# Decoder trunk of two layers: the last expert block chosen by 0/1 products while earlier rows are gathered, and conditioning ahead of the low weight parts at the start

## The chip, the cores and the metric

The kernel runs on one core of a Trainium2 chip. The metric is the device time of one execution in microseconds (us), as the median of several runs. A core has a matrix engine (TensorE, "PE" in the profile, its weight loads "PEld"), three engines for elementwise work (VectorE "DVE", ScalarE "ACT", GpSimd "POOL"), a queue engine (SyncE, "SP") and 16 DMA engines between device memory and the on-chip memory. Every engine runs its own list of instructions in order; they meet only through semaphores.

## The reference

Only what matters here is kept: two layers; each layer conditions its input with a row worked out from `c`, mixes tokens, and then passes them through a feed-forward part, which in the second layer is the mixture of experts.

```python
D_MODEL = 1024; SEQ = 512; DEPTH = 2; N_EXPERTS = 8; TOP_K = 2; D_FF_EXPERT = 1024

def modulate(x, g, shift, scale):
    return rmsnorm(x, g) * (1.0 + scale[:, None, :]) + shift[:, None, :]

def moe_ffn(h, router_w, router_b, w_gate, w_up, w_down):
    t = h.reshape(B * S, D)
    logits = (t @ router_w).astype(jnp.float32) + router_b.astype(jnp.float32)
    top_v, top_i = lax.top_k(logits, TOP_K)
    top_p = jax.nn.softmax(top_v, axis=-1)
    combine = jnp.sum(jax.nn.one_hot(top_i, N_EXPERTS) * top_p[..., None], axis=1)
    for e in range(N_EXPERTS):
        out = out + combine[:, e:e + 1] * swiglu(t, w_gate[e], w_up[e], w_down[e])

def reference(x, c, positions, ada_w, ada_b, ...):
    c_act = jax.nn.silu(c)
    for l in range(DEPTH):
        mod = jnp.einsum('bd,kde->kbe', c_act, ada_w[l]) + ada_b[l][:, None, :]
        ...
        h = modulate(x, norm_mix_g[l], sh1, sc1)
        x = x + gt1 * token_mixer(h, ...)
        h = modulate(x, norm_ffn_g[l], sh2, sc2)
        x = x + gt2 * (swiglu(h, ...) if l % 2 == 0 else moe_ffn(h, ...))
    return rmsnorm(x, final_norm_g)
```

## The kernel before

**Precision.** A float32 product is made of three products of a cheaper type: each operand is split into a high part (a rounded copy, by ScalarE) and a low part (operand minus high part, by VectorE), and TensorE adds high x high, high x low and low x high. The weights are split as they arrive, so each weight tile passes DMA, ScalarE, VectorE and TensorE.

**The opening.** SyncE loads `x`, constants and eight 1 MB groups of `ada` (the conditioning weights), then the first two tiles of `w_in` into `raw`. TensorE multiplies the groups with `cact` as they land (`condition_rows`, line 617, `condition_sum`, line 625); after the eighth, VectorE adds the bias (`modulation`, into `mod` and `sclg`). ScalarE then writes the high part `hhi` of the conditioned `h` and VectorE the low part `hlo`, chunk by chunk (eight chunks of 128 features). VectorE's order is: the low parts of weight tiles 0 and 1 (`split`, line 1755), `modulation`, then eight times {the whole value by line 1850, minus `hhi` by line 1745}. TensorE's `first_pair` (lines 668 to 670) waits for both low weight parts and then follows `h_ready` chunk by chunk, for tiles 0 and 1 together. GpSimd works out rotary angles at the same time (lines 552 to 565).

**The experts.** Each token goes to 2 of 8 experts. VectorE works out for each of the 512 x 2 choices a row number (`slots`) in a buffer `xs` of 15 blocks of 128 rows (NB = 15). GpSimd scatters the token rows there by eight indirect DMAs (line 572), waits for all of them (`xs_done`) and loads block 1 into `xg` (line 575); block 0 is built on the chip by products with 0/1 columns (`first_slots`, line 1183). For each block, TensorE turns `xg` (eight transposes, `slots_in`, line 1210, in the middle of the block before it, at tile t = 20), and works through 24 half-megabyte weight tiles, two at a time (12 pairs): 8 pairs of gate and up products, 4 pairs of down products, 12 products of 128x512 to a pair (lines 1248 to 1250). ScalarE copies the high parts three pairs ahead (`high`, line 1358), but not before TensorE is done with the pair three earlier (`hi_pair` has three places); VectorE follows with the low parts (`low`, into `wlm`). Between them VectorE does `times`, `hidden`, `tokens` and `results`. `results` multiplies the block's output by the gate row `grow` and writes it to `yb`; SyncE stores `yb` to rows of `ys` in device memory (line 502) between the weight loads at t = 20 of the next block, and after the last load for the last block. SyncE's weight loads wait until VectorE is done with the tile twelve earlier.

**The end.** After the last block GpSimd waits for the last store and gathers 2 rows for each token from `ys` by eight indirect DMAs (line 582, into `rawm`, token chunks c = 0 to 3, two each). For each chunk ScalarE multiplies the first row by its share (`weighted`, line 1691), VectorE adds the second times its share (line 1748) and the residual (line 1745, turned into token order by `residual_in_tokens`), ScalarE takes the root (`root`, lines 1697 and 1698), VectorE normalizes (`normed`, lines 2311 and 1748), TensorE turns it back (`out_turned`, line 1257), ScalarE copies it out (`turned_back`, line 1704) and SyncE stores it (line 526).

## Time and profile before

| | us |
|---|---|
| median of 3 runs | 1572.52 |
| lowest and highest of them | 1568.59, 1574.78 |
| the profiled execution's own time | 1571.0 |
| its span, first to last instruction | 1568.9 |

| engine | busy us | share of the span |
|---|---|---|
| PE | 1510.3 | 96% |
| PEld | 1203.1 | 77% |
| DVE | 1161.9 | 74% |
| ACT | 787.1 | 50% |
| POOL | 64.1 | 4% |

The page cuts the span in 40 slices; PE has 5 tenths in the first, 3 in the last and 9 nearly everywhere between. The experts' stage is the stretch from about 1014 us to 1532 us, and what follows it runs to the end at 1568.9. How to read a row of a timeline: start in us, duration in us, engine, line, operation, output<-inputs, shape, how many (merged), and in brackets how long the engine had been idle before it and what ended that.

### The profile page before, as it was taken

The page shows a single profiled execution, that of the slowest core. Times are in us where ns is not written, and L with a number is a line of the kernel's source. Part 1 is how long each engine was busy: PE and PEld are TensorE (multiplying, and loading weights), DVE is VectorE, ACT ScalarE, POOL GpSimd, SP SyncE. Part 2 cuts the span into 40 slices and gives each one's busy share as a digit, 9 for nine tenths or more (in the row PEclk, how much of TensorE's full clock was granted, in tenths as well). Part 3 has the DMA queues.
Part 4 walks back from the last instruction along what each step waited for, and adds up shares of the span by engine and source line. Part 5 has one row for each costly group of instructions (what it writes and reads, how often), then busy time and mean ns, then how long its engine had stood idle before and what let it go on. Part 6 is the DMA issues. An engine that isn't in the chain of part 4 may idle for free.

```text
span 1568.9 us, 22626 instructions
## 1 busy us (share of the span) xinstructions
PE 1510.3 (96%) x9030; PEld 1203.1 (77%) x9030; DVE 1161.9 (74%) x1425; ACT 787.1 (50%) x927; POOL 64.1 (4%) x50
## 2 busy tenths in 40 slices
PE   5999999999999999999999999899999999999993
PEld 3667877778888888886688778688888888888883
DVE  4879866676666665446578765689999999999984
ACT  3534246242222222224542364677777777777774
POOL 8200000000000000000000000200000000000001
PEclk9999999999999999999999999999999999999996
DMA  9453211446555554531211005399999999999975
GB/s 356 138 209 108 82 41 60 155 148 199 187 183 183 185 189 150 183 109 54 68 50 50 26 28 187 112 415 410 396 399 397 400 389 395 393 392 403 397 273 174
DMA packets 94599, 340.33 MB, mean 217 GB/s; under 512 B 10016, under 2 KB 14240, under 8 KB 91808
## 3 DMA queue, kind: packets, MB, share of 16 engines
q1 hardware_dynamic: 92048, 329.99, 57.2%
q0 software_dynamic: 2448, 8.91, 1.5%
q8 instruction: 71, 1.16, 0.3%
q14 instruction: 32, 0.26, 0.0%
HBM read 316.85 MB, written 22.02 MB: 216 GB/s over the span
## 4 chain that ended last, share of the span: by engine, by line
PE 88%; DVE 4%; DMA 4%; issue 1%; ACT 1%; POOL 1%; SPq 0%; POOLq 0%; DVEq 0%; ACTq 0%
PE ps L654 34%; PE ps L1250 10%; PE ps L1248 10%; PE ps L1249 10%; PE ps L964 2%; DMA scr<-in_ada 2%; PE ps L992 1%; DVE scr L1748 1%; PE ps L818 1%; PE ps L810 1%; PE ps L976 1%; DMA xs<-sq,slots 1%; PE ps L606 1%; PE ps L1076 1%; PE ps L1077 1%
## 5 line engine op out<-in xcount | busy, mean ns | idle before, releaser
L1745 DVE TENSOR_TENSOR wlm<-rawm,hlo 128x2048 fp32r<-128x2048 f32 x120 | 274.6, 2289 | 16.8 <-ACT hlo L1358 15.6
L1289 ACT ACTIVATE whi<-raw 128x1024 fp32r<-128x1024 f32 (+1 forms) x112 | 123.6, 1103 | 305.0 <-PE ps L654 260.3
L1358 ACT ACTIVATE hlo<-rawm 128x2048 fp32r<-128x2048 f32 x120 | 230.2, 1919 | 72.2 <-PE ps L1250 72.2
L654 PE MATMUL ps<-hhi,whi 128*128 128x512 f32 x624 | 252.2, 404 | 1.3 <-DVE wlo L1755 1.3
L1755 DVE TENSOR_TENSOR wlo<-raw,whi 128x1024 fp32r<-128x1024 f32 (+1 forms) x112 | 144.1, 1287 | 143.2 <-ACT whi L1289 141.0
L654 PE MATMUL ps<-hlo,whi 128*128 128x512 f32 x624 | 243.6, 390 | 0.0
L654 PE MATMUL ps<-hhi,wlo 128*128 128x512 f32 x624 | 243.6, 390 | 0.0
L1249 PE MATMUL ps<-wlm,xgh 128*128 128x512 f32 x480 | 186.8, 389 | 0.0
L1745 DVE TENSOR_TENSOR wlm<-rawm,whm 128x2048 fp32r<-128x2048 f32 x60 | 137.4, 2291 | 25.7 <-ACT whm L1358 25.7
L654 PEld LDWEIGHTS ps<-hhi,whi 128*128 128x128 f32 x624 | 117.3, 188 | 38.1 <-issue 12.6
L1248 PE MATMUL ps<-hlo,xgh 128*128 128x512 f32 x360 | 141.6, 393 | 1.5 <-ACT xgh L1667 1.5
L1250 PE MATMUL ps<-hlo,xgl 128*128 128x512 f32 x360 | 140.3, 390 | 0.0
L654 PEld LDWEIGHTS ps<-hhi,wlo 128*128 128x128 f32 x624 | 117.3, 188 | 25.7
L654 PEld LDWEIGHTS ps<-hlo,whi 128*128 128x128 f32 x624 | 117.5, 188 | 23.4 <-issue 1.0
L1358 ACT ACTIVATE whm<-rawm 128x2048 fp32r<-128x2048 f32 x60 | 115.0, 1916 | 17.1 <-PE ps L1250 17.1
L1249 PEld LDWEIGHTS ps<-wlm,xgh 128*128 128x128 f32 x480 | 90.2, 188 | 18.3
L1748 DVE SCALAR_TENSOR_TENSOR adas<-adah,cact,adas 128x256 f32<-128x256 f32 x196 | 94.9, 484 | 6.6
L1249 PE MATMUL ps<-wlm,hih 128*128 128x512 f32 x240 | 93.5, 390 | 0.0
L1748 DVE SCALAR_TENSOR_TENSOR scr<-scr,par 128x511 f32<-128x511 f32 (+26 forms) x120 | 82.8, 732 | 1.5
L1248 PEld LDWEIGHTS ps<-hlo,xgh 128*128 128x128 f32 x360 | 67.6, 188 | 15.2 <-ACT xgh L1667 1.6
L1250 PEld LDWEIGHTS ps<-hlo,xgl 128*128 128x128 f32 x360 | 67.6, 188 | 14.3
L654 PE MATMUL ps<-ghi,whi 128*128 128x512 f32 x176 | 69.3, 394 | 0.0
(327 smaller groups left out, 2534.5 us busy)
## 6 DMA issues: line engine op xcount, KB each, us to landing
rawm<-in_wm SPq DMA_DIRECT2D x360, 512.0 KB, 8.0
raw<-in_w SPq DMA_DIRECT2D x96, 512.0 KB, 3.6
adah<-in_ada SPq DMA_DIRECT2D x56, 512.0 KB, 4.4
scr<-in_ada SPq DMA_DIRECT2D x20, 1024.0 KB, 6.0
raw<-in_w SPq DMA_DIRECT2D x16, 704.0 KB, 4.2
xs<-scr SPq DMA_DIRECT2D x15, 512.0 KB, 5.7
ys<-yb SPq DMA_DIRECT2D x15, 512.0 KB, 8.9
xg<-xs SPq DMA_DIRECT2D x13, 512.0 KB, 7.5
```

Of the source, the lines that this page charges most:

```text
L606: ins = pe.matmul(ps[:, 7, 2 * g + m:2 * g + m + 1], ada_sum_in(g)[:, m * P:m * P + P], C("ones")[:, 0:1], start=True, stop=True)
L654: ins = pe.matmul(ps[:, b, :], a, r[:, k0 + k, :], start=(start and first and k == ks[0] and n == 0), stop=(stop and last and k == ks[-1] ...
L810: ins = pe.matmul(ps[cr, 2 + u // 8, u % 8 * 64:u % 8 * 64 + 64], cmp(MT)[cr, u, :], cmp(TC)[cr, u, :], start=True, stop=True)
L964: ins = pe.matmul(ps[:, b, c * 256 + lo:c * 256 + 256], QT[2 * b + c][r, n * P:(n + 1) * P], KT[r, (n - 1) * P + lo:(n + 1) * P], start=Tr ...
L1248: pe.matmul(ps[:, bank, :], ah[:, k, :], w_hi, start=(k == 0), stop=False)
L1249: pe.matmul(ps[:, bank, :], ah[:, k, :], w_lo, start=False, stop=False)
L1250: ins = pe.matmul(ps[:, bank, :], al[:, k, :], w_hi, start=False, stop=(k == DC - 1))
L1289: act.activation(whi[:, slot, 0:width], raw[:, slot, 0:width], ACT.Copy).then_inc(sem("hi_ready"), 1)
L1358: act.activation(hi_pair(q), raw_pair(q), ACT.Copy).then_inc(sem("him_ready"), 1)
L1745: return dve.tensor_tensor(out, a, b, op)
L1748: return dve.scalar_tensor_tensor(out=out, in0=a, scalar=s, in1=b, op0=op0, op1=op1)
L1755: dve.tensor_tensor(wlo[:, slot, 0:width], raw[:, slot, 0:width], whi[:, slot, 0:width].bitcast(F32), ALU.subtract).then_inc(sem("lo_ready ...
```

## The change

There are two parts. In the opening, VectorE does `modulation` first and takes the low part of weight tile 0 behind the first chunk of `hlo` and that of tile 1 behind the second; `first_pair` waits for high and low weight parts where it first uses each. At the end:

- The routing shares are put into slot order, so that `results` can multiply by them: after the eight scatters, GpSimd scatters 8 x 128 single values into `share` (device memory), loads block 1 as before, waits for the shares and loads them as `pslot` (128x16). TensorE's `slots_in(1)` waits for both loads (`xg_first` at 32).
- The last block's rows of `ys` are zeroed at the start of the kernel and never stored. The block before it is stored at t = 13 of the last block instead of t = 20.
- GpSimd gathers as soon as 14 blocks are stored, straight into `htok`, the second row of each token by a DMA that adds.
- The last block's rows are picked on the chip: VectorE makes 0/1 columns (`first_choice`, `second_choice`), TensorE turns them at t = 20, and `rows(c)` adds for each chunk the products `picked` x `yb` and the residual's transposes in the same bank. `combine` is then one addition.

```diff
@@ the sync engine, opening
+                    if t == 0:
+                        sp.dma_start(share.rearrange("(p n) o -> p (n o)", p=P), ZERO[:, 0:16])\
+                            .then_inc(sem("xs_cleared"), 16)
+                        sp.dma_start(ys[(NB - 1) * P:NB * P, :], ZERO).then_inc(sem("xs_cleared"), 16)
@@ the sync engine, expert blocks
-                    if b and t == 20:
+                    if b and t == (20 if b < NB - 1 else 13):
                         store_slots(b - 1)
...
-            store_slots(NB - 1)
@@ gpsimd, after the eight scatters
+            pool.wait_ge(sem("p_ready"), 1)
+            for c in range(4):
+                for k in range(2):
+                    pool.indirect_dma_start(share[:], bass.IndirectOffsetOnAxis(ap=sidx[:, k, c:c + 1], axis=0),
+                                            rt[:, 64 + 4 * k + c:65 + 4 * k + c], None).then_inc(sem("share_out"), 16)
             pool.wait_ge(sem("xs_done"), 8 * 16)
             pool.dma_start(xg[:, 1, :], xs[P:2 * P, :]).then_inc(sem("xg_first"), 16)
-            low_done(pool, NB * NT - 1)
+            pool.wait_ge(sem("share_out"), 8 * 16)
+            pool.dma_start(pslot[:], share.rearrange("(s b) o -> s (b o)", s=P)).then_inc(sem("xg_first"), 16)
             for parity in range(2):
-                pool.wait_ge(sem(f"y_out{parity}"), 16 * ((NB + 1 - parity) // 2))
-            for c in range(4):
-                for k in range(2):
-                    pool.indirect_dma_start(yg[:, c, k, :], None, ys[:],
...
+                pool.wait_ge(sem(f"y_out{parity}"), 16 * ((NB - parity) // 2))
+            for pair in range(2):
+                for k, c in [(k, 2 * pair + q) for k in range(2) for q in range(2)]:
+                    if k:
+                        pool.wait_ge(sem(f"yg_in{c}"), 16)
+                    pool.indirect_dma_start(htok[:, c, :], None, ys[:],
+                                            bass.IndirectOffsetOnAxis(ap=slots[:, k, c:c + 1], axis=0),
+                                            compute_op=ALU.add if k else ALU.bypass).then_inc(sem(f"yg_in{c}"), 16)
@@ tensor, first_pair
-                pe.wait_ge(sem("lo_ready"), g + 2)
...
+                    if k == 0:
+                        pe.wait_ge(sem("hi_ready"), g + j + 1)
                     pe.matmul(ps[:, j, :], w_hi, hhi[:, k, :], start=(k == 0), stop=False)
                     pe.matmul(ps[:, j, :], w_hi, hlo[:, k, :], start=False, stop=False)
+                    if k == 0:
+                        pe.wait_ge(sem("lo_ready"), g + j + 1)
@@ tensor, experts
-                            pe.wait_ge(sem("xg_first"), 16)
+                            pe.wait_ge(sem("xg_first"), 32)
...
                                 if b + 1 < NB:
                                     slots_in(b + 1)
+                                else:
+                                    feature_row(PR("fg", 0, DC), 0)
+                                    slots_turned()
@@ tensor, the end (residual_in_tokens goes)
+                    def rows(c):
+                        for half in range(2):
+                            if c == 0:
+                                pe.wait_ge(sem("y_ready"), NB + half)
+                            pe.matmul(ps[:, 2 * c + half, :], picked[:, c * P:(c + 1) * P],
+                                      yb[:, 0, half * S:(half + 1) * S], start=True, stop=False)
+                            for k in range(4 * half, 4 * half + 4):
+                                ins = pe.matmul(ps[:, 2 * c + half, (k % 4) * P:(k % 4) * P + P],
+                                                x[:, k, c * P:(c + 1) * P], C("ident"), start=False, stop=(k % 4 == 3))
+                        ins.then_inc(sem("htok_done"), 1)
@@ scalar, the end: weighted(c) goes, and turned_rows of the four residual chunks
+                    act.activation(picked, ps[:, 4, :], ACT.Copy).then_inc(sem("htok_ready"), 1)
@@ vector, opening
-            for g in range(2):
-                split(g)
             dve.wait_ge(sem("ada_used"), G_IN)
             modulation(0, 2 * G_IN, 0, 1)
...
+            shifted(0)
             for k in range(DC):
+                if 0 < k < DC - 1:
+                    shifted(k + 1)
                 dve.wait_ge(sem("hhi_ready"), k + 1)
+                tt(hlo[:, k, :], whole(k), hhi[:, k, :].bitcast(F32), ALU.subtract).then_inc(sem("h_ready"), 1)
+                if k < 2:
+                    split(k)
+                if k == 0:
+                    shifted(1)
@@ vector, expert blocks (results, now in stt form with pslot, and the last block)
+                    def last_results(half):
+                        dve.wait_ge(sem("tilem_done"), NT * NB - 2 + 2 * half)
...
+                            if b == NB - 1 and j == 1:
+                                first_choice()
+                            if b == NB - 1 and j == 6:
+                                second_choice()
-                    results(NB - 1)
+                    last_results(0)
+                    last_results(1)
@@ vector, combine(c)
-                        link(stt(y, yg[:, c, 1, :], rt[:, 68 + c:69 + c], y))
-                        tt(y, y, htok[:, c, :], ALU.add).then_inc(sem("z_ready"), 1)
+                        tt(htok[:, c, :], ps[:, 2 * c:2 * c + 2, :].rearrange("p b n -> p (b n)"), htok[:, c, :], ALU.add)\
+                            .then_inc(sem("z_ready"), 1)
```

What stands in a row now, at the three places that matter. First GpSimd's queue (`sq` is the memory of `htok`), from the last scatter on; before:

```order
L572 DMA xs<-sq,slots 1920x1024
L575 DMA xg<-xs 128x1024 [waits xs_done]
L582 DMA rawm<-ys,slots 128x1024 [waits y_out1,y_out0,lom_dve]
L582 DMA rawm<-ys,slots 128x1024 x7
L184 UNCONDITIONAL_BRANCH
```

and now:

```order
L581 DMA xs<-sq,slots 1920x1024
L586 DMA share<-rt,sidx 2048x1 [waits p_ready]
L586 DMA share<-rt,sidx 2048x1 x7
L589 DMA xg<-xs 128x1024 [waits xs_done]
L591 DMA pslot<-share 128x16 [waits share_out]
L599 DMA sq<-ys,slots 128x1024 [waits y_out1,y_out0]
```

Eight more scatters stand between the last row scatter and the load of `xg`, and a second load with a wait of its own behind it.

Second, TensorE behind the last expert product; before:

```order
L1250 MATMUL ps<-whm,hil 128x512
L1173 MATMUL ps<-cst,x 128x128 x16
L1087 MATMUL ps<-cst,par 128x128 x8
L1173 MATMUL ps<-cst,x 128x128 [waits htok_ready]
L1173 MATMUL ps<-cst,x 128x128 x7
```

and now (the pattern of two rows goes on to six pairs before the first L1280 and two more behind it):

```order
L1273 MATMUL ps<-whm,hil 128x512
L1289 MATMUL ps<-yb,xg 128x512 [waits y_ready,htok_ready]
L1292 MATMUL ps<-cst,x 128x128 x4
L1289 MATMUL ps<-yb,xg 128x512 [waits y_ready]
L1292 MATMUL ps<-cst,x 128x128 x4
```

The transposes of the residual have become float32 products that add to the picked rows, and the eight of line 1087 have moved into the last block.

Third, VectorE in the last expert block, from the output of the block before it; before:

```order
L1745 TENSOR_TENSOR yb<-ps,grow 128x1024 [waits y_out1,htok_ready,tilem_done]
L1745 TENSOR_TENSOR wlm<-rawm,hlo 128x2048 [waits tilem_done,him_ready]
L1745 TENSOR_TENSOR wlm<-rawm,whm 128x2048 [waits tilem_done,him_ready]
L1745 TENSOR_TENSOR tm<-sgm,ps 128x512 [waits turn_done,sgm_ready,tilem_done]
L1745 TENSOR_TENSOR wlm<-rawm,hlo 128x2048 [waits tilem_done,him_ready] x2
```

and now:

```order
L1769 SCALAR_TENSOR_TENSOR yb<-ps,pslot,grow 128x1024 [waits y_out1,tilem_done]
L1766 TENSOR_TENSOR wlm<-rawm,hlo 128x2048 [waits tilem_done,him_ready]
L2335 TENSOR_SCALAR pre<-rt 128x8
L2337 TENSOR_SCALAR xg<-iot,pre 128x128 [waits dve_step]
L2337 TENSOR_SCALAR xg<-iot,pre 128x128 x3
L1766 TENSOR_TENSOR wlm<-rawm,whm 128x2048 [waits tilem_done,him_ready]
L1766 TENSOR_TENSOR tm<-sgm,ps 128x512 [waits turn_done,sgm_ready,tilem_done]
```

Five small operations stand between two low parts; four more (`second_choice`) stand further down, between the low part of pair 9 and the second `tm`.

## Rows read from the trace of the kernel before

**Rows 1.** The page: the span.

```profile
span 1568.9 us, 22626 instructions
```

**Rows 2.** Busy time by stretch in blocks 1 to 13: PE, PEld, DVE, ACT, POOL, clock, DMA.

```profile
1060.00:1495.00 435.00, 435.00 (x2021) 361.04 (x2020) 400.84 (x229) 326.38 (x216) 0.00 (x0) 1.00 1.02 398
```

**Rows 3.** Waits of 1040 to 1530: waiting <- released by, us, times, longest.

```profile
PE ps L1210 <- DMA xg<-xs: 0.5, 1, 0.5
```

**Rows 4.** The timeline behind the last expert product.

```profile
1532.11 0.39 PE L1250 MATMUL ps<-whm,hil 128*128 128x512 f32 x1
...
1537.18 1.00 POOL L582 DMA_INDIRECT rawm<-ys,slots  x1 [500.37 <-DMA ys<-yb]
...
1543.79 1.15 ACT L1691 ACTIVATE rawm<-rawm,rt 128x1024 f32<-128x1024 f32 x1 [6.55 <-DMA rawm<-ys,slots]
...
1557.71 1.22 DVE L1745 TENSOR_TENSOR rawm<-rawm,sq 128x1024 f32<-128x1024 f32 x1
...
1560.70 1.28 DVE L1748 SCALAR_TENSOR_TENSOR rawm<-rawm,rt,frow 128x1024 f32<-128x1024 f32 x1
...
1564.10 1.02 ACT L1704 ACTIVATE x<-ps 128x1024 f32<-128x1024 f32 x1 [0.68 <-PE ps L1257]
```

**Rows 5.** Timelines of TensorE: float32 products and transposes of the same shapes.

```profile
1004.17 9.00 PE L1183 MATMUL ps<-xg,sq 128*128 128x128 f32 x64 [1.21 <-ACT sq L1636]
...
712.46 1.02 PE L639 MATMUL ps<-sq,cst 128*128 128x512 f32 x2
...
1532.34 1.91 PE L1173 MATMUL ps<-cst,x 128*128 128x128 f32 x16
```

**Rows 6.** Timelines of the last block, and VectorE's 128x128 columns in the routing.

```profile
1509.22 2.28 DVE L1745 TENSOR_TENSOR wlm<-rawm,whm 128x2048 fp32r<-128x2048 f32 x1
...
1522.70 0.68 DVE L1745 TENSOR_TENSOR tm<-sgm,ps 128x512 f32<-128x512 f32 x1
...
1523.70 0.60 PE L1218 MATMUL ps<-cst,tm 128*128 128x128 f32 x4
...
1509.89 1.92 ACT L1358 ACTIVATE hlo<-rawm 128x2048 fp32r<-128x2048 f32 x1 [0.80 <-PE ps L1250]
...
1507.13 0.41 SPq L502 DMA_DIRECT2D ys<-yb  x1
...
1002.08 1.15 DVE L1748 SCALAR_TENSOR_TENSOR xg<-ps,logit 128x128 f32<-128x128 f32 x4 [0.93 <-PE ps L1200]
```

**Rows 7.** Chain of waits: the last scatter to its landing, and the load of xg.

```profile
1020.38 15.56 DMA xs<-sq,slots
...
1036.22 7.31 DMA xg<-xs
```

**Rows 8.** DMA queues (packets, MB, share of 16 engines) in 1026 to 1031.

```profile
q1 hardware_dynamic: 289, 1.05, 51.5%
q0 software_dynamic: 287, 1.04, 51.1%
```

**Rows 9.** GpSimd's queue in 1034 to 1036, then in 1036 to 1040.

```profile
q0 software_dynamic: 3, 0.00, 0.6%
...
q0 software_dynamic: 2, 0.01, 0.5%
```

**Rows 10.** The DMA view of 4 to 4.5 us: many packets under 512 B.

```profile
DMA packets 148, 0.09 MB, mean 177 GB/s; under 512 B 84, under 2 KB 130, under 8 KB 148
...
q1 hardware_dynamic: 148, 0.09, 84.8%
```

**Rows 11.** Timelines of the opening, and its clock (columns as in rows 2).

```profile
34.35 2.17 ACT L1289 ACTIVATE whi<-raw 128x1024 fp32r<-128x1024 f32 x2
...
35.44 2.92 DVE L1755 TENSOR_TENSOR wlo<-raw,whi 128x1024 fp32r<-128x1024 f32 x2 [2.43 <-ACT whi L1289]
...
41.35 0.56 PE L668 MATMUL ps<-hhi,whi 128*128 128x512 f32 x1 [2.72 <-DVE hlo L1745]
...
52.15 0.69 DVE L1745 TENSOR_TENSOR hlo<-scr,hhi 128x512 fp32r<-128x512 f32 x1
...
41.30:44.80 3.50, 3.45 (x8) 2.45 (x9) 3.43 (x4) 3.50 (x6) 3.33 (x3) 0.54 0.82 332
```

More of the change, by code:

```diff
@@ L254, in trunk @@
             slots = sb("slots", [2, 4], I32, stack=room)
+            sidx = sb("sidx", [2, 4], I32, stack=room)
+            pslot = sb("pslot", [16], stack=room)
+            iot = sb("iot", [P], stack=room)
             grow = sb("grow", [D], stack=room)
@@ L257, in trunk @@
         ys = nc.dram_tensor("ys", (NB * P, D), F32, kind="Internal").ap()
+        share = nc.dram_tensor("share", (16 * P, 1), F32, kind="Internal").ap()
         def rawm_tile(g):
@@ L279, in trunk @@
         yg = rawm[:].rearrange("p g n -> p (g n)")[:, 0:8 * D].rearrange("p (c k d) -> p c k d", c=4, k=2)
+        last_hot = xg[:, 1, 0:4 * P].rearrange("p (c s) -> p c s", c=4)
+        picked = xg[:, 1, 4 * P:8 * P]
         sqj = rawm[:].rearrange("p g n -> p (g n)")[:, 8 * D:9 * D]
@@ L1168, in token_major, with slots_turned @@
                         token_half(c, 1)
[L1170 to L1174 removed]
+                    def slots_turned():
+                        pe.wait_ge(sem("sel_ready"), 5)
+                        for c in range(4):
+                            ins = pe.transpose(ps[:, 4, c * P:(c + 1) * P], last_hot[:, c, :], C("ident"))
                         ins.then_inc(sem("htok_done"), 1)
@@ L1259, in out_turned @@
                         ins.then_inc(sem("out_turned"), 1)
-                    residual_in_tokens(0)
-                    residual_in_tokens(1)
-                    feature_row(PR("fg", 0, DC), 0)
-                    for c in (2, 3):
-                        pe.wait_ge(sem("htok_ready"), 4 + c)
-                        residual_in_tokens(c)
-                    pe.wait_ge(sem("htok_ready"), 10)
-                    for c in range(4):
+                    def rows(c):
[8 more added lines that the diff above has]
+                        ins.then_inc(sem("htok_done"), 1)
+                    pe.wait_ge(sem("htok_ready"), 7)
+                    rows(0)
+                    rows(1)
+                    rows(2)
+                    out_turned(0)
+                    rows(3)
+                    for c in range(1, 4):
                         out_turned(c)
@@ L2273, in _ @@
                     link(dve.reciprocal(rt[:, 64:68], four(3)))
-                    tt(rt[:, 68:72], four(2), rt[:, 64:68]).then_inc(sem("p_ready"), 1)
+                    link(tt(rt[:, 68:72], four(2), rt[:, 64:68]))
+                    low7 = pre[:, 0:8].bitcast(I32)
+                    high = pre[:, 8:16].bitcast(I32)
+                    flat = slots[:].rearrange("p k c -> p (k c)")
+                    link(dve.tensor_scalar(low7, flat, P - 1, 4, ALU.bitwise_and, ALU.logical_shift_left))
@@ L2279, in results @@
                         if b >= 2:
                             dve.wait_ge(sem(f"y_out{b % 2}"), 16 * (b // 2))
-                        tt(yb[:, b % 2, :], ps[:, 6:8, :].rearrange("p b n -> p (b n)"), grow[:])\
-                            .then_inc(sem("y_ready"), 1)
+                        stt(yb[:, b % 2, :], ps[:, 6:8, :].rearrange("p b n -> p (b n)"), pslot[:, b:b + 1], grow[:],
+                            ALU.mult, ALU.mult).then_inc(sem("y_ready"), 1)
+                    def last_results(half):
+                        dve.wait_ge(sem("tilem_done"), NT * NB - 2 + 2 * half)
+                        dve.wait_ge(sem("y_out0"), 16 * (NB // 2))
+                        stt(yb[:, 0, half * S:(half + 1) * S], ps[:, 6 + half, :], pslot[:, NB - 1:NB], grow[:, half * S:(half + 1) * S],
+                            ALU.mult, ALU.mult).then_inc(sem("y_ready"), 1)
@@ new lines, in first_choice, with second_choice @@
+                    def first_choice():
+                        at = pre[:, 0:8]
+                        link(dve.tensor_scalar(at, rt[:, 72:80], -float((NB - 1) * P), None, ALU.add))
+                        for c in range(4):
+                            ins = dve.tensor_scalar(last_hot[:, c, :], iot[:], pre[:, c:c + 1], None, ALU.is_equal)
+                        ins.then_inc(sem("sel_ready"), 1)
+                    def second_choice():
+                        dve.wait_ge(sem("sel_ready"), 4)
+                        for c in range(4):
+                            ins = stt(last_hot[:, c, :], iot[:], pre[:, 4 + c:5 + c], last_hot[:, c, :], ALU.is_equal, ALU.add)
+                        ins.then_inc(sem("sel_ready"), 1)
```

56 lines of the change are left out of this document (23 added, 33 removed).

## The prediction

> **What bounds the kernel now.** I read the page first, then busy time by stretch, then the waits, then the timelines of the three places that the change touches. The profiled execution took 1571.0 us, of which the span is 1568.9 [rows 1]; the sum below is made against 1571.0, which lies 1.5 under the median of 1572.5. A measurement of this kernel can tell about 0.5% (7.9 us) from no change. In the experts' blocks TensorE is busy for all of 435 us, and the DMA engines are full beside it [rows 2]. In this whole stage it waited once, for `xg` of block 1, 0.5 us long [rows 3]: so whatever comes later there is paid in full, and nothing behind it gives it back. Outside that stage the change touches two stretches in which TensorE isn't the bound: the end, where the last product starts at 1532.11 and the span goes on to 1568.9 through store, gather and four chunks of elementwise work [rows 4], and the opening.
>
> **The end: about 7.9 us off.** Before, from the end of the last product (1532.5) to the end of the span are 36.4 us. Now the store and the gather's 6.55 us wait are gone, because GpSimd's gathers need only block 13 stored. Their cover: block 13's output is stored from 1507.1 [rows 6]; a pair of gathers lands some 6.6 us after the first is issued [rows 4], and there are four such rounds in a row (row, added row, for each pair of chunks), so the first two chunks are complete near 1526 and the last near 1540, against needs at about 1540 and 1548. A round would have to take twice as long before this cover fails. What is late next is TensorE: `rows(c)` is two float32 products of 128x512 (two instructions of 0.43 us each, as 1.02 us for the two with the drain shows) and eight of 128x128 (9.00 us for 32 of them: 0.28 each) [rows 5], so 2 x 0.86 + 8 x 0.28 = 4.0 us a chunk. With `out_turned(0)` (eight transposes, 1.0 us) between, `rows(3)` ends 4 x 4.0 + 1.0 = 17.0 us behind the last expert product. Then `combine(3)` 1.3; root, reciprocal and normalizing: from the end of the addition at 1558.9 to the end of normalizing at 1562.0 is 3.05 us; ScalarE now does `turned_back(1)` ahead of `root(3)`, 0.9 more; eight transposes and their drain 1.3, copy 1.0, store to the end of the span 3.8 [rows 4]. Sum: 17.0 + 1.3 + 3.05 + 0.9 + 1.3 + 1.0 + 3.8 = 28.4, so 36.4 - 28.4 = 8.0; I take 7.9, since the first `rows` waits a moment for `picked` and `yb`. The first half of `yb` is made while the last tiles run, and the second half is ready before TensorE comes to it.
>
> **The last block: about 3.1 us on.** (a) Twelve transposes (line 1087's eight, four of the 0/1 columns) are now in front of the last products: at 1.91 us for 16 [rows 5], 1.4 us. Before, the eight lay in the shadow of the store. (b) `first_choice` is one tiny operation and four of 128x128. VectorE's four such took 1.15 us [rows 6]; from memory on the chip rather than PSUM perhaps 0.7, so 0.9 to 1.3. It pushes the low part of pair 5, which ended at 1511.50, while TensorE came to pair 5 at about 1512.4 (ScalarE was released at 1509.89 by the end of pair 3, and a pair takes 2.7): 0.3 us of stall, between 0 and 0.6. (c) `second_choice`, 1.0 (0.8 to 1.3), stands right ahead of the second `tm`, which ended at 1523.38, 0.3 before the turn that needs it [rows 6]: with the delay already there about 1.1 of stall, between 0.4 and 1.6. (d) The store at t = 13 holds SyncE until `yb` is written (1507.1) with the loads of tiles 13 to 19 behind it; ScalarE wanted tile 13 at 1509.89 [rows 6]. A load out of an empty queue would land near 1511.3, after the store's half megabyte; that falls into the delay of (b) for the most part: 0.3, between 0 and 1.5. Together 1.4 + 0.3 + 1.1 + 0.3 = 3.1, between 1.8 and 5.
>
> **The opening: nothing.** TensorE may start some 3 us earlier than 41.35, but it follows VectorE's `hlo` chunks, the last of which began at 52.15. VectorE waited until 35.44 for the first high weight part [rows 11]; now it waits for the conditioning sums at nearly the same time (the copy that releases the last of them ends when the first `split` of ScalarE begins, 34.35). Its list is as long as before, only in another order, so the last chunk of `hlo` comes at the same time. Bounds: 1 us off for waits that the new order fills, 0.5 on for the first chunk of `hhi`, which follows ScalarE's second `split` at 36.5 [rows 11]. SyncE's two more writes are half a megabyte in a stretch where the tiles aren't wanted before 53.9. I take 0.
>
> **The shares: 13.6 us on.** This is the term that decides. Eight scatters of 128 four-byte values are queued behind the row scatters in GpSimd's queue. Issuing them costs nothing, since GpSimd only waited there; the last row scatter, issued at 1020.38, landed 15.56 us later [rows 7], because its packets were in line. The two queues took turns packet by packet: 289 to 287 in 5 us, which is 16 x 5 / 576 = 0.139 us a packet on one engine [rows 8]. By 1034 GpSimd's queue had only 3 packets left [rows 9], and the completion was seen at 1035.9, 1.9 later. Now 8 x (8 + 1 for the completion) = 72 packets for each engine come next. A small packet costs about 0.85 x 16 x 0.5 / 148 = 0.046 us [rows 10], but if each still waits for one of the weights' 4 KB packets, a turn is 0.139 + 0.046 = 0.185 and the 72 take 13.3 us. So: values moved at 1047.3, `share_out` seen at 1049.2, `pslot` issued at 1049.5; the load of `xg` moved its first packets only 3.8 us after its issue (2 packets up to 1040, issued at 1036.22) [rows 7, 9], so 1053.3, nine turns 1.7, landing at 1055.5. TensorE wanted `xg` at 1043.0: a stall of 12.5, less the 0.5 that it had [rows 3], is 12.0. After such an idle stretch the clock is down: in the opening the granted clock was 0.54 (near 1.2 of 2.4 GHz) for 3.5 us, in which eight products ran that need 1.9 at the full one [rows 11], so 1.6 more. Low end: the small packets go through at once, `xg` lands as before and `pslot` with it, 0. High end: a small write costs as much as a 4 KB packet, 72 x 0.278 = 20.0 instead of 13.3, so 18.7 + 1.6 = 20.3. I take the middle value because rows 8 are the nearest: same queues, same moment, same turns.
>
> The Trainium skill, "DMA: Bandwidth & Descriptors", section "Queues, rings and completion order", says that an engine round-robins between its queues by packet, and that a packet may hold several descriptors (typically 9 to 17). Rows 8 can't tell this from turns of single descriptors, as both queues then moved 4 KB rows. By the page the nine small ones of a scatter could go in one turn; that is the second rival below.
>
> **Sum.** 1571.0 - 7.9 + 3.1 + 0 + 13.6 = 1579.8, that is 0.5% over the median: the gain at the end is eaten in block 0.
>
> **Rivals.**
> 1. *Slower: small writes to device memory cost as much as long ones.* 20.3 instead of 13.6: 1586.5. It decides as soon as shares and clock together cost over 14.2, which is the point where the total passes 1580.4; a small packet of 0.055 us rather than 0.046 is enough. For it: nothing in the trace writes four bytes in such numbers. Against: the completions are small writes too, and they didn't hold up the scatters. (The same page of the Trainium skill, section "Specifications", says that below 512 B the engine reads and writes back; no row here shows the price.)
> 2. *The small packets of a scatter share a turn.* Eight turns of 0.139 + 9 x 0.046 = 0.55 are 4.4 us: values moved at 1038.4, seen at 1040.3, `pslot` issued 1040.6, moving at 1044.4, landing near 1045.3. Stall 1.8 more than before, no loss of clock: 1571.0 - 7.9 + 3.1 + 1.8 = 1568.0. Against it: the counts of rows 8, read plainly.
> 3. *Faster: the shares cost nothing and VectorE's slack in the last block swallows the choices.* Only the twelve transposes are left: 1571.0 - 7.9 + 1.4 = 1564.5, or lower with 1 us from the opening. It needs two low ends at once.
> 4. *The opening gains what it seems to.* If the rotary work on GpSimd disturbs VectorE less in the new order, TensorE's earlier start could give up to 3 us. It shifts each case and stands in the range.
>
> **How the numbers follow.** The forecast (about 1576 to 1584, by the bounds of the other terms) has a chance of 0.50, rival 2 (1565 to 1572) 0.25, rival 3 0.12, rival 1 0.13. The predicted time is the forecast's, 1579.8. The range leaves out the outer half of rivals 1 and 3: 1565 to 1587. The median before is 1572.5, so faster by over 0.5% is under 1564.7, slower over 1580.4. Faster: rival 3 with a little of rival 2, 0.15. Slower: rival 1 and nearly half of the forecast, 0.35. Within: 0.50.
>
> **What would show it.** In the profile after, TensorE's wait ahead of the first transposes of `xg`, released by the load of `pslot`: 12 us by the forecast, 2 by rival 2, none by rival 3, 19 by rival 1; and the clock behind it. The stretch from the last expert product to the end: 28 to 29 us. The last block: two stalls of TensorE, at pair 5 and at the second turn, about 1.7 together, and `y_ready` 3 us later relative to the block's start. The opening: the last `hlo` at 52 to 53. The prediction is wrong if the first of these is small, if the adding gathers take twice the plain ones and hold up `combine`, or if `rows` isn't at 4.0 us a chunk because the clock has fallen.

## The result, and the profile after

The changed kernel took 1586.22 us (median of 7 runs, 1581.61 to 1587.53), the kernel before in the same comparison 1574.78 (7 runs). The ratio is 1.0078, with a 95% interval of 1.0062 to 1.0093: slower by 0.8%, or 11.4 us, where 1579.8 (8.8 over the 1571.0 that the sum started from) and no measurable change were forecast. The profiled execution took 1587.21 us. Its page (span; busy time and share by engine) stands beside [rows 1] and the table of engines:

```profile
span 1585.4 us, 22738 instructions
...
PE 1526.9 (96%) x9082; PEld 1213.5 (77%) x9082; DVE 1158.8 (73%) x1434; ACT 779.9 (49%) x921; POOL 90.9 (6%) x59
...
q0 software_dynamic: 2736, 8.93, 1.8%
```

GpSimd is busy for 27 us more, with only the shares' nine further transfers; that is the first hint. Set against each other, the two traces give the span's 16.5 us as follows (a place is found in both by the same instruction):

| stretch | before | after | change |
|---|---|---|---|
| start to the first expert product | 1014.6 | 1019.2 | +4.5 |
| to the first transposes of `xg` | 1043.6 | 1057.0 | +8.9 |
| to the transposes ahead of the last block | 1492.4 | 1507.7 | +1.9 |
| to the end of the last expert product | 1532.5 | 1559.1 | +11.3 |
| to the end of the span | 1568.9 | 1585.4 | -10.1 |

This pair of executions lies 5 us further apart than the medians (16.5 against 11.4), and the first row is where such scatter sits: in the eleven profiles of this document that have the old opening, the first expert product came between 1011.9 and 1020.7 us; in the three with the new one between 1019.2 and 1022.4. The other four rows come to 12.0.

TensorE's waits between 1000 and 1590 (waiting <- released by, us, times, longest); before, the place of the first row shown cost 0.5 [rows 3], and the other two weren't there:

```profile
PE ps L1230 <- DMA pslot<-share: 9.4, 1, 9.4
PE ps L1271 <- DVE wlm L1766: 4.8, 2, 2.7
...
PE ps L1238 <- DVE tm L1766: 2.0, 1, 2.0
```

**The shares.** GpSimd's timeline from the first row scatter on, with the issue of each transfer as its duration:

```profile
1016.78 0.95 POOL L581 DMA_INDIRECT xs<-sq,slots  x1 [0.30 <-issue]
...
1027.65 2.83 POOL L586 DMA_INDIRECT share<-rt,sidx  x1 [0.30 <-issue]
1030.79 2.02 POOL L586 DMA_INDIRECT share<-rt,sidx  x1 [0.30 <-issue]
...
1038.54 0.95 POOL L586 DMA_INDIRECT share<-rt,sidx  x1 [0.30 <-issue]
...
1044.47 2.50 POOL L586 DMA_INDIRECT share<-rt,sidx  x1 [0.30 <-issue]
1046.97 0.61 POOL L589 DMA_DIRECT2D xg<-xs  x1
1051.58 0.58 POOL L591 DMA_DIRECT2D pslot<-share  x1 [4.00 <-DMA share<-rt,sidx]
```

The eight issues take from 1027.65 to 1046.97, 19.3 us, and the load of `xg` stands behind them. It left 10.8 us later than before [rows 7], while TensorE was 4.5 us later. It took 7.5 us, so `xg` was there near 1054.5; the last 2.5 us of TensorE's wait are those of `pslot`, whose load had to wait for the last scatter. What VectorE did beside the issues tells why they took so long:

```profile
1027.36 2.29 DVE L1766 TENSOR_TENSOR wlm<-rawm,hlo 128x2048 fp32r<-128x2048 f32 x1 [0.83 <-ACT hlo L1391]
1029.68 2.29 DVE L1766 TENSOR_TENSOR wlm<-rawm,whm 128x2048 fp32r<-128x2048 f32 x1
...
1038.73 2.29 DVE L1766 TENSOR_TENSOR wlm<-rawm,whm 128x2048 fp32r<-128x2048 f32 x1 [0.72 <-ACT whm L1391]
```

The issue of 1027.65 began while the first of these subtractions ran and ended 0.83 us behind its end (1029.65); that of 1030.79 began in the second and ended 0.84 behind it. Seven of the eight issues go like this, 0.82 to 0.84 behind. The eighth, of 1038.54, began 0.19 us ahead of a subtraction and took 0.95.

TensorE then ran at half clock for a while (granted clock, the column behind the five busy times, 0.69 from 1057 to 1062):

```profile
1057.00:1062.00 5.00, 4.98 (x20) 4.34 (x21) 1.23 (x1) 1.02 (x1) 0.00 (x0) 0.69 0.96 382
```

**The last block.** SyncE's queue, then two rows of ScalarE, which makes the high weight parts:

```profile
1495.28 17.41 SPq L500 DMA_DIRECT2D rawm<-in_wm  x13
1522.45 0.33 SPq L512 DMA_DIRECT2D ys<-yb  x1
1522.97 7.09 SPq L500 DMA_DIRECT2D rawm<-in_wm  x11
...
1529.19 1.92 ACT L1391 ACTIVATE hlo<-rawm 128x2048 fp32r<-128x2048 f32 x1 [4.84 <-DMA rawm<-in_wm]
...
1551.74 1.91 ACT L1391 ACTIVATE whm<-rawm 128x2048 fp32r<-128x2048 f32 x1 [4.58 <-DMA rawm<-in_wm]
```

SyncE stood at the store from 1512.7 to 1522.45 and issued no weights; ScalarE waited 4.84 us for the first tile behind it. In [rows 6] the store (then at t = 20) was issued at once. With the gathers beside them, the eleven last loads took a median of 12.1 us from issue to landing. The last one took longest; it is in the chain that ended last, and the 4.58 us wait above is for it:

```profile
1529.74 21.93 DMA rawm<-in_wm
```

**The end.** TensorE behind the last expert product, and the last steps:

```profile
1558.91 1.02 PE L1289 MATMUL ps<-yb,xg 128*128 128x512 f32 x2
1559.77 1.05 PE L1292 MATMUL ps<-cst,x 128*128 128x128 f32 x8
...
1562.41 1.02 PE L1289 MATMUL ps<-yb,xg 128*128 128x512 f32 x2
...
1580.77 1.02 ACT L1732 ACTIVATE x<-ps 128x1024 f32<-128x1024 f32 x1 [1.95 <-PE ps L1280]
```

From the end of the last expert product (1559.1) to the end of the span it is 26.3 us, against 36.4 before [rows 4]. No `combine` waited for a gather.

### The profile page after: what moved, and what is told of

It reads as the page before. It is cut to its first block, busy times and chain, and to the rows that moved or that the text cites. A ratio compares the mean times of both kernels' runs of the same rounds, so it can differ in the third digit from the quotient of the medians.

```text
span 1585.4 us, 22738 instructions
## 1 busy us (share of the span) xinstructions
PE 1526.9 (96%) x9082; PEld 1213.5 (77%) x9082; DVE 1158.8 (73%) x1434; ACT 779.9 (49%) x921; POOL 90.9 (6%) x59
## 4 chain that ended last, share of the span: by engine, by line
PE 87%; DVE 4%; DMA 4%; POOL 2%; issue 1%; ACT 1%; SPq 1%; DVEq 0%; ACTq 0%; POOLq 0%
PE ps L671 34%; PE ps L1271 9%; PE ps L1273 9%; PE ps L1272 9%; PE ps L984 2%; DMA scr<-in_ada 2%; PE ps L1012 1%; DMA rawm<-in_wm 1%; DVE scr L1769 1%; PE ps L838 1%; PE ps L830 1%; PE ps L996 1%; POOL share L586 1%; PE ps L623 1%; PE ps L1096 1%
```

## The experiments

Ratios are to the kernel before, with 95% intervals. "Last block" is the time from the transposes in front of it to the end of the last expert product, in the profile (before 40.1, after 51.4); "tail" is what follows.

**The opening alone.** The kernel before, with VectorE's new order and TensorE's later waits.

```diff
-            for g in range(2):
-                split(g)
...
+                if k < 2:
+                    split(k)
```

> The kernel before with only the opening's new order (modulation first, the two low weight parts behind the first two chunks, first_pair waiting where it uses them). Theory from the two traces: the new order costs something, because TensorE starts early, stalls once for the low part of tile 1, falls to half clock and itself becomes the bound of the first pair: 1.9 us at the first short convolution, and 4.7 us from 208 us on, so about 1577.5 against 1572.5 to 1575. Rival: only the 1.9 belong to the opening and the other 2.8 (a stretch of half-clock products near 100 to 114 us) fell by chance: about 1.9 over the kernel before. The prediction: no difference.

1.0012 (0.9999 to 1.0025), 1573.86 us. The opening costs little: 1.9 us, and that it costs nothing can't be excluded. The 4.5 us of the profile of after don't belong to it in full. In its profile TensorE's first product for the gates starts at 56.3 (before 55.1, after 56.9).

**The end alone.** The changed kernel with the old opening; all that follows is built on it.

```diff
+            for g in range(2):
+                split(g)
...
-                if k < 2:
-                    split(k)
```

> The changed kernel with the old opening, so the end and the shares alone. If the opening costs 4.7 us: 1586.2 - 4.7 = 1581.5. If it costs 1.9: 1584.3. If nothing: 1586. The wait of TensorE ahead of the first transposes of xg (9.4 us) and the stalls of the last block should be as in the changed kernel.

1.0074 (1.0054 to 1.0094), 1582.94 us. So nearly all of the loss is in the shares and the end. Last block 49.6, tail 25.6, wait for `pslot` 9.3.

**Without the share scatters.**

```diff
-            for c in range(4):
-                for k in range(2):
-                    pool.indirect_dma_start(share[:], ...).then_inc(sem("share_out"), 16)
...
-            pool.wait_ge(sem("share_out"), 8 * 16)
```

> As e2_end, but the eight scatters of the shares and the wait for them are left out (pslot is then loaded as zeros, so the experts' part of the output is missing). Theory: GpSimd needs 19.3 us to issue the eight scatters, and this puts off the load of xg and that of pslot; without them the wait of 9.4 us and the half clock behind it go, 10.8 us less than e2_end, and TensorE waits at most 1 us for pslot. Rival: the second load with its own round trip of 5.4 us is what holds TensorE; then 4 to 5 us of wait stay and the gain is near 6. Everything behind that place should stay as in e2_end.

0.9997 (0.9983 to 1.0011), 1572.57 us: 10.4 us less than the end alone by the medians (12.1 by the ratios), as expected, and TensorE doesn't wait at all for the second load. The rival falls. The page counts what the eight scatters were to the DMA engines. Queue 0 of this kernel (packets, MB, share of 16 engines):

```profile
q0 software_dynamic: 2480, 8.92, 1.8%
```

That is 256 packets fewer than in after's page above, 2 for each scatter and engine, where I had counted 9.

**VectorE with one input.** The disputed cost by itself: is it the packets or the issuing, and what makes issuing long?

```diff
+                if 0 <= q < 13:
+                    dve.tensor_scalar(lo_pair(q), raw_pair(q), 0.0, None, ALU.mult).then_inc(sem("lom_dve"), 1)
+                else:
                     tt(lo_pair(q), raw_pair(q), hi_pair(q).bitcast(F32), ALU.subtract).then_inc(sem("lom_dve"), 1)
```

> As e2_end, but the low parts of the first thirteen pairs of the experts' weights are written by VectorE as raw x 0 (one tensor read from on-chip memory instead of two; the part of the products that rests on these low parts is left out). VectorE should be busy for about as long an instruction (2.1 to 2.3 us), so only the number of tensors that it reads changes. Theory: GpSimd's issue of a scatter waits until an instruction of VectorE with two inputs in on-chip memory has ended; then the eight share scatters go from 2.0 to 2.8 us each to 0.95, the eight take 10 us instead of 19.3, the load of xg goes out when the row scatters have landed, TensorE's wait of 9.3 us shrinks to about 1 to 3 us, and the time is 6 to 9 us under e2_end's 1.0074 of before. Rival: GpSimd is slowed by any work of VectorE (or by something else), the scatters stay at 2.0 to 2.8 us and the time stays.

1.0044 (1.0029 to 1.0059), 1578.07 us. Its timelines of GpSimd and VectorE:

```profile
1020.31 0.96 POOL L586 DMA_INDIRECT share<-rt,sidx  x1 [0.66 <-DVE sidx L1763]
1021.57 1.38 POOL L586 DMA_INDIRECT share<-rt,sidx  x1 [0.30 <-issue]
...
1021.58 1.25 DVE L1880 TENSOR_SCALAR wlm<-rawm 128x2048 fp32r<-128x2048 f32 x1 [1.55 <-ACT hlo L1388]
...
1031.39 0.96 POOL L586 DMA_INDIRECT share<-rt,sidx  x1 [0.30 <-issue]
1034.63 0.59 POOL L589 DMA_DIRECT2D xg<-xs  x1 [2.28 <-DMA xs<-sq,slots]
1038.98 0.76 POOL L591 DMA_DIRECT2D pslot<-share  x1 [3.76 <-DMA share<-rt,sidx]
```

The eight issues take 12.0 us instead of 19.3, the load of `xg` waits only for the row scatters, and TensorE's transposes follow without a wait. The packets are the same 256, so packets weren't the cost. But my expectation that VectorE would be busy as long was wrong: 1.25 us instead of 2.29. Issues are still held by the one-input instruction: the three that had begun up to 0.27 us before it ended 0.12 us behind its end (the one of 1021.57 is shown), and one that began during it (1027.62) ended 0.82 behind. So this run shows that issuing follows what VectorE runs at that moment, not that the second input is what matters; the issues are shorter because the instruction is. And only 4.7 us came back: the last block took 54.0 in this profile (54.4 in that without shares, 49.6 in the end alone). In all three SyncE stood 9.8 us at the store of block 13. So part of a stall that goes in block 0 can be lost again in the last block; why, the runs don't settle.

**Block 13 stored at t = 20 again.**

```diff
-                    if b and t == (20 if b < NB - 1 else 13):
+                    if b and t == 20:
```

> As e2_end, but block 13's output is stored at t = 20 of the last block again instead of t = 13. Theory S: the last block's 11.3 us come mainly from SyncE, which waits for yb with seven loads behind the store; then the stalls of ScalarE for weights and of TensorE in the last block nearly go, about 7 us less than e2_end, as the gathers still start some 10 us ahead of the last expert product. Theory G: they come mainly from the gathers' 4 MB that take turns with the weights; then the first stall goes, the later ones stay, and the gain is 0 to 3 us, or the end gets longer because the gathers land later.

1.0020 (1.0007 to 1.0034), 1575.15 us: 7.8 less. Last block 42.7, tail 26.4. One wait is left, ahead of the second turn, and the end is none the later for it:

```profile
PE ps L1235 <- DVE tm L1763: 0.6, 1, 0.6
```

This supports theory S, but the gathers also started later, 2.7 us behind SyncE's last issue of a weight load, so this run can't tell the store from the gathers.

**Gathers held until the last weight tile has landed**, the store still at t = 13.

```diff
+            g = NB * NT - 1
+            pool.wait_ge(sem(f"landed{g % RING}"), 16 * (LANDED_BEFORE[g % RING] + g // RING + 1))
```

> As e2_end (store at t = 13, SyncE held by it), but GpSimd starts its gathers only when the last weight tile has landed. Theory S (the store that holds SyncE costs most of the last block's 11 us): the first stall of ScalarE for weights (4.6 us) stays, so the last block stays long, gain 0 to 3 us over e2_end's 1582.9. Theory G (the gathers' 4 MB in turns with the weights): ScalarE's later waits (1.5, 2.4, 3.1 us) and TensorE's stalls behind the first go, 4 to 7 us less. In both the gathers then run beside fewer transfers, and the tail may grow if they end too late (more than 26 us from the last expert product to the end). GpSimd should issue a gather in 0.95 to 3.6 us, long ones where VectorE subtracts two tiles in on-chip memory.

1.0049 (1.0033 to 1.0065), 1579.37 us. Last block 45.1; the later waits of ScalarE shrink, the first (4.4 us) stays. About 3.6 us, between the theories.

**Block 13 stored by GpSimd**, so that SyncE never waits for it.

```diff
-                    if b and t == (20 if b < NB - 1 else 13):
+                    if b and b < NB - 1 and t == 20:
...
+            pool.wait_ge(sem("y_ready"), NB - 1)
+            pool.dma_start(ys[(NB - 2) * P:(NB - 1) * P, :], yb[:, (NB - 2) % 2, :]).then_inc(sem("xg_first"), 16)
```

> As e2_end, but block 13's output is stored from GpSimd's queue as soon as it is there, so SyncE never waits; the gathers start as early as before or earlier. Theory S: ScalarE's waits for weights go, the last block takes 42 to 43 us from the last transposes of xg to the last product instead of 49.6, about 1576. Theory G: the gathers now compete with still more of the weights, and the block stays at 48 or more, about 1582.

1.0024 (1.0014 to 1.0034), 1575.08 us. Last block 42.8: 7.9 us less than the end alone, with the same 4 MB of gathers. Together ("hold" is SyncE standing at the store of block 13; last block in us): hold and gathers 49.6, hold alone 45.1, gathers alone 42.8, neither (in "all three together" below) 42.7. The held SyncE costs 2.4 us by itself, and both together 6.9, up to 11.7 in the other profiles that have both (51.4 to 54.4): each makes the other dear. That gathers cost nothing is shown only for weights that are ahead of them: here, against what was expected, they began later (22.8 us into the last block instead of 18.5), because GpSimd's store took 7.2 us to land, and SyncE had issued its last weight load 1.6 us before. Gathers beside weights that are still to be issued, with SyncE never stopped, were not run.

**Half the shares ahead of `xg`, half behind it.** TensorE waits for `xg` alone; VectorE's first use of `pslot` is moved to the fifth pair of block 1.

```diff
-            for c in range(4):
+            for c in (0, 1):
                 for k in range(2):
                     pool.indirect_dma_start(share[:], ...).then_inc(sem("share_out"), 16)
             pool.wait_ge(sem("xs_done"), 8 * 16)
             pool.dma_start(xg[:, 1, :], xs[P:2 * P, :]).then_inc(sem("xg_first"), 16)
+            for c in (2, 3):
...
-                            if j == 0 and b:
+                            if b and j == (4 if b == 1 else 0):
                                 results(b - 1)
```

> As e2_end, but only four of the eight share scatters stand ahead of the load of xg, the other four and the load of pslot behind it; TensorE's transposes wait for xg alone, and VectorE's results(0), the first use of pslot, is moved from the first to the fifth pair of block 1. Theory: the wait of 9.3 us and the half clock behind it go, because GpSimd issues four scatters (10 us) in the 12 us in which it only waited for the row scatters: 10 to 11 us less than e2_end's 1582.9, so about 1572.5. Rival: the four small scatters' packets or their completions keep the load of xg back in GpSimd's queue, 2 to 5 us of wait stay; or pslot comes after results(0) needs it, near 1059, and TensorE stalls at the second half of block 1 instead.

1.0034 (1.0020 to 1.0049), 1577.67 us: 5.3 less than the end alone, half of what was expected. The wait for `xg` is gone, but a new one of 1.7 us came at 1083, and the last block took 54.0.

**All three together**: GpSimd's store, the held gathers and the reordering.

> The changes of e6_reorder, e8_poolstore and e5_hold together (old opening, xg ahead of half the shares, block 13 stored by GpSimd, gathers after the last weight tile has landed). If the shares' stall (10.8 us) and the last block's stalls (7 us) can both be had back and the gathers still end in time: 1582.9 - 10.8 - 7 = 1565, about 7 us less than the kernel before. If the held gathers end too late, the tail grows from 26 us by what they are late.

0.9997 (0.9983 to 1.0010), 1570.18 us: 4 to 5 us short. Last block 42.7 and tail 26.2 are as wanted. SyncE's queue in block 1 shows what is missing, then the clock, DMA share and GB/s (last three columns) of 1065 to 1070, and ScalarE:

```profile
1055.85 3.52 SPq L500 DMA_DIRECT2D rawm<-in_wm  x4
1070.64 0.33 SPq L512 DMA_DIRECT2D ys<-yb  x1
...
1065.00:1070.00 5.00, 5.00 (x26) 4.14 (x25) 4.65 (x3) 4.09 (x4) 0.00 (x0) 1.00 0.17 69
...
1077.49 1.92 ACT L1397 ACTIVATE hlo<-rawm 128x2048 fp32r<-128x2048 f32 x1 [4.46 <-DMA rawm<-in_wm]
```

My own reordering had made the same fault as the change: SyncE stood 11 us at a store whose `yb` now came late, and the DMA engines ran dry.

**The store of block 0 moved too**, and `results(0)` to the second pair.

```diff
-                    if b and b < NB - 1 and t == 20:
+                    if b == 2 and t == 2:
+                        store_slots(0)
+                    if 1 < b < NB - 1 and t == 20:
                         store_slots(b - 1)
...
-                            if b and j == (4 if b == 1 else 0):
+                            if b and j == (1 if b == 1 else 0):
```

> As e7_pool, but results(0) stands behind the second pair of block 1 instead of the fifth, and SyncE stores block 0's output at t = 2 of block 2. In e7_pool SyncE stood at the store of block 0 until 1070.6 (12 us later than in the kernel before), the DMA engines fell to a share of 0.17 in 1065 to 1070, and TensorE then waited 2.6 us; from the first transposes of xg to those of the last block it took 454.0 us instead of 448.8. Theory: that was the same fault as the store at t = 13 (SyncE waits, the weights behind it), so 449 to 450 us come back and the time is 4 to 5 us under e7_pool's 1570.2, near 1565.5. Rival: the time went into the half clock behind the wait for xg (2 us) and the rest is spread over the blocks; then at most 1 to 2 us come back.

0.9961 (0.9948 to 0.9974), 1565.75 us: 4.4 less than without by the medians (5.7 by the ratios, as the kernel before was itself measured anew), as the theory said; the stretch from the first transposes of `xg` to those of the last block went from 454.0 to 449.5. The DMA engines' share in 1065 to 1070 is back at 1.03:

```profile
1065.00:1070.00 5.00, 4.95 (x25) 3.78 (x24) 5.00 (x4) 3.12 (x3) 0.00 (x0) 1.00 1.03 408
```

**The same without holding the gathers.**

```diff
-            g = NB * NT - 1
-            pool.wait_ge(sem(f"landed{g % RING}"), 16 * (LANDED_BEFORE[g % RING] + g // RING + 1))
```

> As e9_best, but the gathers start as soon as block 13 is stored instead of behind the last weight tile. If the weights are ahead enough, their turns with the gathers cost nothing, as in e8_poolstore: the same time as e9_best. If holding them was worth something, 1 to 3 us more, in waits of ScalarE for weight tiles in the last block.

0.9952 (0.9935 to 0.9970), 1565.49 us; last block 42.7 again, no wait of ScalarE for a weight tile in it. Holding is worth nothing. This version and the one above are faster than both kernels: 0.4 to 0.5% under the kernel before, 1.2% under the changed one. TensorE's waits in its experts' stage, where after had 9.4, 4.8 and 2.0:

```profile
PE ps L1236 <- DMA xg<-xs: 0.6, 1, 0.6
PE ps L1244 <- DVE tm L1772: 0.6, 1, 0.6
```

**The opening with both low parts behind the first chunk.**

```diff
-                if k < 2:
-                    split(k)
                 if k == 0:
+                    split(0)
+                    split(1)
                     shifted(1)
```

> The kernel before with the opening's new order, but with both low weight parts behind the first chunk of hlo (instead of one behind each of the first two). Theory: in the new order TensorE is the bound of the first pair from the moment when the low part of tile 1 is there (44.6 us), in half clock at first; with it some 1.6 us earlier, the first pair ends about 1 us earlier than in e1_opening (where the first products of the gates start at 56.3, against 55.1 before), if the later chunks of hlo don't take over as the bound. Rival: VectorE's chunks are the bound; then it ends as in e1_opening or later. In the median both are hard to see: e1_opening was 0.1% over the kernel before.

1.0006 (0.9993 to 1.0019), 1574.97 us; the median tells nothing. In the profile my theory fails: the low part of tile 1 is there at 42.9, 1.7 us sooner, and the gates start at 57.3, 1 us later. TensorE now waits for the second chunk:

```profile
42.89 0.49 PE L673 MATMUL ps<-hhi,wlo 128*128 128x512 f32 x1 [1.29 <-DVE wlo L1758]
46.17 0.79 PE L669 MATMUL ps<-hhi,whi 128*128 128x512 f32 x1 [2.79 <-DVE hlo L1748]
```

What the three new orders share is a wait of TensorE that ends late, at 44.5, 44.6 and 46.2, and 11.2 to 12.3 us of uninterrupted products from there to the gates, the first ones at half clock. Before, the last long wait ended at 41.35 [rows 11]. That this is the cause is read from the profiles and not tested by itself.

## Why the prediction was right and wrong

**The shares: the size near by luck, the mechanism wrong.** 13.6 was forecast, 8.9 + 1.9 = 10.8 read from the trace, 10.4 measured by taking them out; TensorE's wait was 9.4, against 12 forecast. The step "Issuing them costs nothing, since GpSimd only waited there" failed. Behind the last block, beside an idle VectorE, an issue takes 1.00 us [rows 4]; here, beside VectorE's subtractions, most took 2.0 to 2.8, which added up to 19.3 us where GpSimd had been idle for 13.4 us. I had read where GpSimd waits, but not how long its issues take there; this row of the kernel before, the issue of its last row scatter, would have told it:

```profile
1020.38 2.42 POOL L572 DMA_INDIRECT xs<-sq,slots  x1 [0.30 <-issue]
...
1036.22 0.58 POOL L575 DMA_DIRECT2D xg<-xs  x1 [13.43 <-DMA xs<-sq,slots]
```

It too began while a subtraction (1019.67 to 1021.96) ran. The other half, 72 packets in turns of 0.185 us, failed too: there were 16 for each engine, so rival 2's eight turns were nearer, and its time (1568.0) didn't come because the issuing took the packets' place. The loss to the clock was right: 1.6 forecast, 1.9 in the trace.

**The last block: the term that decided.** 3.1 was forecast, 11.3 came. It is why a change clear of noise came where none was forecast. Of it, (a) to (c) are right in sum: with SyncE free the block takes 42.7 or 42.8, so 2.6 to 2.7 over 40.1, against 2.8 forecast. The four 128x128 operations of `first_choice` measured 0.88, and the 1.1 us ahead of the second turn were 0.6. The step that failed is (d), "0.3, between 0 and 1.5". I asked when the first load behind the store would land, out of an empty queue. The right question was how long SyncE issues nothing: it comes to a block's stores when `yb` has just been written, and t = 13 is seven tiles earlier than t = 20, 7 x 1.36 = 9.5 us (half of a pair's 2.7 each); it stood 9.8. The loads then went out all at once, in turns with 4 MB of gathers that I had only set against their own need, and not against the weights' queue. Taking the hold away gave back 7.8 us with the store at t = 20 and 7.9 with GpSimd storing; holding the gathers back, with SyncE's stop left in, gave 3.6.

**The end: right, 2.2 us low.** 7.9 off was forecast, 10.1 came. `rows(c)` is 3.5 us, not 4.0: the eight instructions from 1559.77 to 1560.65 are four 128x128 products, so one takes 0.22 and not the 0.28 of [rows 5]; four chunks with 0.5 less are 2.0 of the 2.2. The adding gathers held nothing up, even at 9.4 us a landing.

**The opening: right within the measurement.** The last `hlo` ended at 52.2 (before 52.8), as forecast, but in the profile TensorE had become the bound behind it. The new opening cost 1.9 and 0.9 us by the ratios of the two kernels that have it alone, and 0.6 from the end alone to the changed kernel, none clear of its interval. That TensorE could lose by starting earlier, and stopping, wasn't among the rivals.

**The sum.** Forecast were 13.6 + 3.1 - 7.9 = 8.8 us on; the trace has 10.8 + 11.3 - 10.1 = 12.0, and the medians 11.4. (The two profiled executions also differ by the 4.5 of the first stretch, which lies inside the scatter of that stretch.) The 8.2 that the forecast had too little for the last block were in part covered by 2.8 too much for the shares and 2.2 too little gained at the end. The time lay inside the range and near the end of rival 1 (1586.5), but by another mechanism; that is luck.

## What to carry to other kernels

Before moving a store or any waiting instruction in a queue that also feeds the bound, count the work behind it: the queue stands still for the distance moved times its pace (9.5 us worked out here, 9.8 measured), not for one transfer's latency. What the bound then pays depends on what else is in the DMA engines: 2.4 us of the last block without the gathers, 6.9 and more with them. The same fault came back in a mend, because `yb` was made later instead of the store being put earlier. And an engine that seems to have time for more issues must be costed at the duration that an issue takes at that very place, beside what the other engines do there (2.41 us for each of the eight here, with the gaps, where 1.25 was the pace beside an idle VectorE).

## What the hardware showed that I had not expected

GpSimd needs 0.95 us to issue an indirect transfer of 128 rows or 128 single values, and 1.55 for a gather that adds. What matters is the instruction of VectorE that is running when the issue begins. If it is a subtraction of two tensors in on-chip memory (2.29 us), the issue ends 0.82 to 0.88 us behind the end of that subtraction (109 of 113 such issues in the fourteen traces; 1.42 to 1.49 behind it for nearly all of those that add), so it takes up to 3.1 us, or 3.7 if it adds. If a subtraction starts 0.05 us or more after the issue, the issue isn't held (0.95 to 1.01 us, 37 times); the one exception, of 3.24 us in the kernel where GpSimd stores block 13, began less than 0.1 us ahead of the second of two subtractions in a row. The one-input instruction of the experiment does hold an issue that has just begun. One that began while `tm<-sgm,ps` ran, which takes one input from PSUM (after, 1545.32), took 0.95 as well.

The Trainium skill, "SBUF — State Buffer", section "SBUF: two separate sides", says that VectorE and GpSimd share a pair of ports as an exclusive lock, and calls a GpSimd transfer that waits for its descriptors the "DVE blocks DMA" trap. The trace agrees in that an issue waits for one instruction to end, with the numbers above; the section tells of the trap for instructions in a mode that takes both ports, and here issues are held beside the two-input subtraction too. It would have been a reason to doubt the prediction's free issues.

The eight scatters of 128 four-byte values were 2 packets for each engine and scatter, so several values travel in one packet; the Trainium skill, "DMA: Bandwidth & Descriptors", section "Queues, rings and completion order", which lets a packet hold several descriptors, was right against my count of nine packets.
